# ScalarE takes half of the softmax division, and two first taps of a convolution; the sink maximum becomes one operation

## The reference, cut to what matters

```python
s = einsum(q, k) * scale ; s = where(valid, s, -inf)         # 128 queries x 256 keys in each block of 128 tokens
probs = softmax(concatenate([s, sink], axis=-1))[..., :-1]   # sinks: one number for each query head
o = einsum(probs, v)
...
qkv = silu(causal_conv(concatenate([q, k, v]), conv_w))      # DeltaNet: 4 taps along the tokens, per channel
```

## Time and profile before

| | before |
|---|---|
| median of 3 runs | 2521.81 us (2514.71 to 2522.38) |
| the profiled execution, its own time | 2521.18 us |
| its span, first to last instruction | 2519.4 us |
| mean granted TensorE clock | 0.987 |
| TensorE busy | 2390.0 us (95%) |
| VectorE busy | 1881.2 us (75%) |
| ScalarE busy | 943.3 us (37%) |
| GpSimd busy | 1071.2 us (43%) |

### The profile page before, as it was taken

One profiled execution on the slowest core, in us unless ns is written; L12 is line 12 of the kernel. 1 busy time (PEld: TensorE's weight loads), 2 busy tenths in 40 slices (PEclk: granted clock), 3 DMA queues, 4 the chain that ended last, 5 costly groups with the idle time before them and its releaser, 6 DMA issues. The chain is left out here.

```text
span 2519.4 us, 38470 instructions
## 1 busy us (share of the span) xinstructions
PE 2390.0 (95%) x15284; PEld 1899.3 (75%) x15284; DVE 1881.2 (75%) x2356; ACT 943.3 (37%) x1488; POOL 1071.2 (43%) x675
## 2 busy tenths in 40 slices
PE   8887999899999999999999999999999999999997
PEld 6655777687788877888777778777777888778885
DVE  3676666646878889888947677777568877988887
ACT  3154223214433334443514244444253333443433
POOL 3411222233555555454544433343445555555542
PEclk9998999999999999999999999999999999999998
DMA  4200000211244375434112111111314344644332
GB/s 162 68 17 17 27 27 27 80 48 42 103 173 147 138 246 182 157 126 167 42 65 95 53 34 35 35 35 43 117 34 147 138 146 162 244 167 151 131 123 99
DMA packets 109709, 254.99 MB, mean 101 GB/s; under 512 B 9312, under 2 KB 9568, under 8 KB 107360
## 3 DMA queue, kind: packets, MB, share of 16 engines
q1 hardware_dynamic: 104112, 233.82, 27.3%
q10 hardware_dynamic: 5424, 18.75, 2.2%
HBM read 182.28 MB, written 67.63 MB: 99 GB/s over the span
## 5 line engine op out<-in xcount | busy, mean ns | idle before, releaser
L681 PE MATMUL pairs<-x_hi,w_hi 128*128 128x512 f32 x1592 | 545.2, 407 | 36.5 <-DVE x_lo L1755 16.4
L681 PE MATMUL pairs<-x_lo,w_hi 128*128 128x512 f32 x1592 | 530.6, 397 | 0.8 <-issue 0.8
L681 PE MATMUL pairs<-x_hi,w_lo 128*128 128x512 f32 x1592 | 527.7, 396 | 0.8 <-issue 0.8
L681 PEld LDWEIGHTS pairs<-x_hi,w_hi 128*128 128x128 f32 x1592 | 286.9, 190 | 118.8 <-issue 37.8
L645 POOL TENSOR_TENSOR idle<-idle 128x1 f32<-128x1 f32 x78 | 19.5, 250 | 781.7 <-PE pairs L681 772.2
L681 PEld LDWEIGHTS pairs<-x_hi,w_lo 128*128 128x128 f32 x1592 | 299.4, 190 | 64.4 <-issue 0.9
L681 PEld LDWEIGHTS pairs<-x_lo,w_hi 128*128 128x128 f32 x1592 | 298.3, 190 | 62.9 <-issue 1.3
L664 POOL TENSOR_TENSOR w_lo<-w_raw,w_hi 128x512 fp32r<-128x512 f32 x150 | 238.1, 1596 | 230.1 <-ACT w_hi L1278 230.0
L681 PE MATMUL pairs<-work_r,w_hi 128*128 128x512 f32 x1072 | 329.9, 391 | 4.8 <-DVE work_r L1751 2.1
L681 PE MATMUL mid<-work_r,w_hi 128*128 128x512 f32 x992 | 309.6, 393 | 17.8 <-DVE work_r L1751 12.1
L664 POOL TENSOR_TENSOR w_lo<-work,w_hi 128x512 fp32r<-128x512 f32 x128 | 178.0, 1392 | 216.7 <-ACT w_hi L1278 216.7
(11 more groups left out here) (217 smaller groups left out, 3920.9 us busy)
## 6 DMA issues: line engine op xcount, KB each, us to landing
h_ops<-work SPq DMA_DIRECT2D x224, 256.0 KB, 4.4
w_raw<-w_stream SPq DMA_DIRECT2D x81, 512.0 KB, 3.5
w_raw<-w_up SPq DMA_DIRECT2D x120, 256.0 KB, 3.8
out_sq<-h_ops SPq DMA_DIRECT2D x28, 1024.0 KB, 5.2
x_lo_raw<-h_ops SPq DMA_DIRECT2D x28, 1024.0 KB, 5.1
work<-w_down SPq DMA_DIRECT2D x16, 1024.0 KB, 6.8
out_sq<-w_down SPq DMA_DIRECT2D x8, 1024.0 KB, 7.3
x_lo_raw<-w_down SPq DMA_DIRECT2D x8, 1024.0 KB, 5.5
```

The source lines that it names most:

```text
L681: return nc.tensor.matmul(out, w, x, start=start, stop=stop)
```

## The change

Four edits.

1. `masked_max`: the negated sinks are prepared once (`SINK_NEG`, 8 numbers a row). The bias is then one operation, min(-maximum, -sink), in place of two; the sink term is sink plus bias. VectorE has two small operations for a group in place of three.
2. `normalize`: VectorE multiplies only the first two of the four heads (`BY_DVE = 2`, 128x512). ScalarE multiplies the other two in `norm_rest(i)`, one operation of 128x256 each with the reciprocal as its scale, put ahead of `probs_t(i)` in ScalarE's order. It waits for the reciprocals (`s_rec`), and `probs_transposed(i)` waits for it (`s_max2`).
3. ScalarE makes the first taps of `conv(0, 0)` and `conv(0, 1)` (`first_tap`), between norm_rest(15) and probs_t(15).
4. The second tap of `conv(0, 0)` on VectorE moves ahead of the last `take`; `conv` is defined earlier for that.

```diff
+        SINK_NEG = stat[:, 0:QH]
+        BY_DVE = 2
@@ TensorE: probs_transposed(i)
                 pe.wait_ge(s["p_norm"], i + 1)
+                pe.wait_ge(s["s_max2"], 1 + (GRP - BY_DVE) * (i + 1))
@@ ScalarE
+            def norm_rest(i):
+                act.wait_ge(s["s_rec"], i + 1)
+                rec = 16 + 24 * (i % 3) + 20
+                for j in range(BY_DVE, GRP):
+                    a(att_probs(i)[:, j, :], att_probs(i)[:, j, :], ACT.Copy, s["s_max2"], scale=stat[:, rec + j:rec + j + 1])
+
+            def first_tap(n):
+
+                act.wait_ge(evacuated, V_DN + n + 1)
+                a(CONV[n], HEAD0[n], ACT.Copy, s["s_exp"], scale=par[:, P_CONV + 4 * n + 3:P_CONV + 4 * n + 4])
             exps(0)
             exps(1)
             for i in range(CH * KVH):
+                norm_rest(i)
+                if i == CH * KVH - 1:
+                    act.wait_ge(s["s_psum"], CH)
+                    first_tap(0)
+                    act.wait_ge(s["s_masked"], CH * KVH)
+                    first_tap(1)
                 probs_t(i)
@@ VectorE: masked_max(i)
-                tt(mx, mx, sink, ALU.max, s["s_max2"])
-                dve.wait_ge(s["s_max2"], i + 1)
-                nc.vector.tensor_scalar(stat[:, st:st + 4], mx, -1.0, None, ALU.mult).then_inc(s["s_bias"], 1)
-                tt(stat[:, st + 8:st + 12], sink, mx, ALU.subtract, s["s_bias"])
+                nc.vector.scalar_tensor_tensor(stat[:, st:st + 4], mx, -1.0, SINK_NEG[:, kv * GRP:(kv + 1) * GRP],
+                                               ALU.mult, ALU.min).then_inc(s["s_bias"], 1)
+                dve.wait_ge(s["s_bias"], 2 * i + 1)
+                tt(stat[:, st + 8:st + 12], sink, stat[:, st:st + 4], ALU.add, s["s_bias"])
@@ VectorE: normalize(i)
-                tt(sc, sc, along(rec, 2 * P), ALU.mult, s["p_norm"])
+                tt(sc[:, 0:BY_DVE, :], sc[:, 0:BY_DVE, :], along(rec[:, 0:BY_DVE], 2 * P), ALU.mult, s["p_norm"])
+            nc.vector.tensor_scalar(SINK_NEG, par[:, P_SINK:P_SINK + QH], -1.0, None, ALU.mult).then_inc(s["s_max2"], 1)
             dve.wait_ge(s["masks_in"], 16)
+            dve.wait_ge(s["s_max2"], 1)
@@ VectorE: conv
+                    by_act = h == 0 and ahead == 0 and n < 2 and j == 1
+                    if by_act:
+                        dve.wait_ge(s["s_exp"], (GRP + 1) * CH * KVH + n + 1)
+                    else:
+                        dve.wait_ge(s["conv"], bump(h, 12, 12 * ahead + 4 * n + j))
-                                                   ALU.mult, ALU.add).then_inc(s["conv"], 1)
+                                                   ALU.mult, ALU.add).then_inc(s["conv"], 2 if by_act else 1)
@@ VectorE: behind the loop
+            conv(0, 0, HEAD0, taps=(1,))
             take(V_DN + 3, 0, HEAD0[3])
             dve.wait_ge(s["pt_psum"], CH * KVH)
...
-            conv(0, 0, HEAD0)
+            conv(0, 0, HEAD0, taps=(2, 3))
...
-                    conv(0, 1, raw)
+                    conv(0, 1, raw, taps=(1, 2, 3))
```

More of the change, by code:

```diff
@@ L1857, in _, with conv, tap @@
             take(V_DN, 0, HEAD0[0])
+            def conv(h, n, raw=A, ahead=0, taps=range(4)):
+                src, dst = raw[n], CONV[n]
+                def tap(j):
+                    return par[:, bass.ds(P_CONV + h * 12 + ahead * 12 + n * 4 + j, 1)]
+                if 0 in taps:
+                    dve.wait_ge(evacuated, V_DN + h * 4 + ahead * 4 + n + 1)
+                    nc.vector.tensor_scalar(dst, src, tap(3), None, ALU.mult).then_inc(s["conv"], 1)
+                for j in taps:
+                    if j == 0:
+                        continue
+                    by_act = h == 0 and ahead == 0 and n < 2 and j == 1
[3 more added lines that the diff above has]
+                        dve.wait_ge(s["conv"], bump(h, 12, 12 * ahead + 4 * n + j))
+                    nc.vector.scalar_tensor_tensor(dst[:, j:], src[:, :SEQ - j], tap(3 - j), dst[:, j:],
+                                                   ALU.mult, ALU.add).then_inc(s["conv"], 2 if by_act else 1)
             last_fill = {att_fill(n, part): KVH * n + min(part, 1) for n in range(CH) for part in range(ATT_PARTS)}
```

## The result

| | before | after |
|---|---|---|
| median of 9 runs each | 2522.38 us (2514.71 to 2525.79) | 2529.63 us (2525.15 to 2535.79) |
| the profiled execution, its own time | 2521.18 us | 2527.46 us |
| its span | 2519.4 us | 2525.3 us |
| mean granted TensorE clock | 0.987 | 0.986 |

The ratio after to before is 1.0038, with a 95% interval of 1.0028 to 1.0048. The changed kernel is slower, by 0.38% or 9.6 us (the medians of the table differ by 7.3). The time lies in the predicted range and 4.6 us above the forecast. The prediction gave 0.69 to "same", a change under 0.3%, and 0.22 to "slower"; 0.38% is on the slower side of that bound, with an interval that begins at 0.28%.

What follows compares the result with a forecast made beforehand. It expected odd transposes to wait for ScalarE, whose exponentials precede its division. Terms +6.2 +1.3 -2.0 -2.0 -1.9 -1.0 +3.0 = +3.6 on 2521.18 us gave 2524.8; with the median 0.6 higher, 2525 us, range 2516 to 2533.

Steps and rivals of the forecast that it cites:

- What bounds the stage: Attention rounds: odd transposes would wait for ScalarE, whose exponentials precede norm_rest; TensorE stands 2.5 us, some 2 us a round.
- The round: Undisturbed attention rounds: 12.93 us in place of 10.88; +6.2 over blocks 1 to 4 and +1.3 in block 6.
- Block 0: First attention block: shorter by 2.0 us (-0.5 to -2.45), with earlier second transposes and a smaller TensorE hole.
- Block 5: Attention block 5: shorter by 2.0 us (-0.5 to -3.6), transposes at V+12.4, or 13.4 if caught by GpSimd.
- The end: Block 6's `values` to the first sums of squares: 21.8 to 23.6 us against 24.56, taken as -1.9 (-1.0 to -2.8).
- The clock in the rounds: TensorE at half clock after the new 2.5 us holes in two of five rounds, 1.5 each: +3.0 us (0 to +7.5).
- Half clock in most rounds: Attention rounds: a listed sign that the prediction is wrong, TensorE at half clock in most of them.
- The clock behind the end: Behind the 7.39 us hole, shrunk to 2 to 4: better TensorE clock gives back 1.0 us (0 to -2.5).
- The sum: Whole kernel: all terms together give +3.6 us, on the profiled 2521.18 us, forecast 2525 us.
- The held-up bias operation: Rival, blocks 0 and 5: GpSimd's L646 holds up VectorE's new bias operation; about 2528 us, chance 0.12.
- VectorE as the bound: Rival, attention rounds: VectorE's chain stays the bound and ScalarE's two heads are hidden; -15 us, 2507, chance 0.06.
- The clock rival: Rival: clock falls in all rounds and stays low in blocks 0 and 5; +10 us, 2532, "slower", chance 0.22.

Runs made afterwards that it cites:

- the kernel with the division ahead: The changed kernel with norm_rest(i + 1) put ahead of exps(i + 2) in ScalarE's order; 2511.93 us, ratio 0.9963 to before.
- the kernel with group 1 only: The changed kernel with ScalarE dividing two heads of group 1 alone, VectorE all other groups whole; 2510.39 us, ratio 0.9959 to before.
- the filled hole: The changed kernel with ten unread 128x512 matmuls ahead of each odd group's transposes in blocks 0 to 6; 2524.14 us, ratio 1.0011 to before.
- the division alone: The kernel before with edit 2 only, ScalarE dividing two heads of each group; 2537.86 us, ratio 1.0053 to before.
- the bias alone: The kernel before with edit 1 only, the single bias operation; 2518.15 us, ratio 0.9986 to before.
- all but the division: The changed kernel with VectorE dividing all four heads again, edits 1, 3 and 4 kept; 2512.19 us, ratio 0.9958 to before.
- the taps alone: The kernel before with edits 3 and 4 only, VectorE dividing all four heads; 2517.01 us, ratio 0.9984 to before.
- the kernel before with filled holes: The kernel before with unread 128x512 matmuls, 14 ahead of group 1's transposes and 22 ahead of group 11's; 2514.75 us, ratio 0.9975 to before.

## Why the prediction was right, and where it missed

- **What bounds the stage.** Right. TensorE's odd transposes wait for ScalarE, 2.62 us (forecast some 2), with VectorE's half done 1.8 before ScalarE's begins.
- **The round.** Right: even transposes at V+5.53 (5.50), odd ones at V+10.61 (10.52), 13.00 (12.93), two multiplications 0.90 (0.90). When the prediction set 0.90 beside the trace's 1.23 it was still an estimate; measured now, it agrees. Blocks 1 to 4 as a chain: 4 x 13.00 - 45.56 = +6.4 (forecast +6.2), block 6 +1.4 (+1.3). The proof that the order is the cause is the kernel with the division ahead.
- **Block 0.** -2.48 (forecast -2.0, bound -2.45). GpSimd's two-input operation, at 121.08, ended 4.40 behind the first transposes and not 5.16 as before, so the half division that it caught (2.66 long) ended at 123.98, just as ScalarE's chain did; behind the 2.62 hole the clock stayed full here. What the forecast did not have is why GpSimd was earlier: VectorE's half division of group 0, as the kernel with group 1 only shows.
- **Block 5.** -2.02 (-2.0), transposes at V+12.40 (12.4). From there to `values` 3.98, at reduced clock; behind the filled hole it was 2.39. The gain is the other edits': without the division the block takes 14.92, so the division costs here too.
- **The end.** -2.22 (-1.9), sums 22.34 behind `values` (22 to 24). The odd transposes came at V+9.42 and not 8.45, because TensorE was at low clock behind its hole of 2.00 (even transposes 1.54); with the holes filled it is V+8.55. The taps made -5.2 alone, and the division's later `values` took 3.0 back.
- **The clock in the rounds: the term that was mis-sized.** The forecast put two of five rounds at half clock, 1.5 each: +3.0. The profile has three of five, 1.50, 1.42 and 1.38: +4.3. The profile with filled holes has 6.7 for the clock of the whole stage. "Half clock in most rounds" stood among the signs of being wrong, and three of five is most: by its own sign this part of the forecast failed.
- **The clock behind the end: the other one.** The forecast took back 1.0. From the sums to the next transposes were 13.11 (234.51 to 247.62) against 12.90: +0.2. The hole ahead of the sums shrank from 7.39 to 2.01, but the clock behind it was no better: 0.66 over these 13.11 us, with TensorE busy 10.38, against 0.75 over the 12.90 and 9.59 before. With the holes filled the same way took 12.09 at 0.86.
- **The sum.** The stage has +5.4 and the way from the sums to the next transposes +0.2, 5.6 against 3.6. That is 2.0 more, all in the two clock terms (1.3 and 1.2, less 0.5 from the others). The profiled executions differ by 6.3 and the ratio says 9.6, 2.7 times the forecast's 3.6; that the time still lies 4.6 from the forecast and in the range is owed in part to a range of 17 us. (The terms at their ends, -4 and +13, make 2518 to 2535 from the median before and not the 2516 to 2533 written; 2529.6 lies in both.) Where 9.6 less 6.3 comes from is open. Behind the stage the two profiles drift against each other in work that the change did not touch: GpSimd's markers of the changed kernel are 4.0 later than those of before at 599, 9.9 later at 1755, and 8.2 later at 1859. So a single pair of profiles is good to a few us over the whole kernel, and the spread of the runs (2525 to 2536, and 2515 to 2526 before) needs no rounds at half clock to explain it.
- **The rivals.** The held-up bias operation fell: it ran at 190.55 in 0.16, inside GpSimd's L649 (188.99 to 191.76), though both its inputs are in SBUF. The Trainium skill's rule (SBUF — State Buffer, Who interferes with whom) isn't borne out for this pair; for the two-input L651 it is, with 2.66 for a half division. The trace of before had this already: inside L646 (182.70 to 185.47) the maximum with the sink, with two SBUF inputs, took 0.16 at 184.26, and the operation held for 1.03 was L1840, which has one. At the taps both sides lost: three took 4.57 where one takes 1.29, and GpSimd's L649 took 3.81 and not 2.77. VectorE as the bound fell with the chain of waits. The clock rival came in part: three of five rounds and not all, and block 0 at full clock. Its word, "slower", is where the measured ratio lies.

## What to carry to other kernels

On an engine that runs its queue in order, a moved operation costs what stands ahead of it: the same two multiplications a group (0.90 us) on an engine 62% idle made a round 13.00 behind four exponentials and 11.23 ahead of them, against 10.8 without. Before moving work to the idle engine, put its slot on the timeline beside the moment the consumer wants it, and try the other slots. Then count what the new hole does to TensorE's clock; if the hole must stay, a few matmuls that nobody reads can be cheaper than the low clock behind it.

## What was unexpected

- The same hole of 2.62 us was followed by half clock at 150.10 (transposes 1.94) and by full clock at 137.10 (1.07), in rounds with the same instructions. I found no row that tells them apart beforehand; rounds alternated in this profile and in that of the division alone. The length of the hole alone does not decide: behind 3.81 us in block 0 the eight transposes took 1.13 in the kernel before and 1.09 with the bias alone, but 1.97 in all but the division and with the taps alone; behind 1.90 they took 1.63 in the kernel before with filled holes, and 1.09 behind 1.91 without.
- Matmuls without use lowered the ratio three times: by 0.27% on the change, 0.25% on the kernel before, 0.22% on the one with group 1 (0.9959 to 0.9937, whose intervals overlap).
- A VectorE operation of half the size, caught by GpSimd's two-input operation, took 2.66 where the whole took 3.12: halving it saved 0.46 of its own 0.54 (1.23 less 0.69), and nothing of the wait.
